# Taps in two halves, an earlier Sin, and four products per state block for the last four tiles of an S5 layer

## The reference, cut to what matters

```python
# 64 groups of 16 channels, 64 complex states per group
ab = exp(lam * dt);  bb = f * b                # zero-order hold
bu = einsum('blgp,gnp->blgn', u, bb)
st = scan of  s[t] = ab * s[t-1] + bu[t]       # complex, over 256 tokens
y  = einsum('blgn,gpn->blgp', st_re, cr) - einsum('blgn,gpn->blgp', st_im, ci)
y  = y + d_skip * h
g  = gelu(y);  out = g * sigmoid(g @ w_glu + b_glu)
```

## Time and profile before

| what | value |
|---|---|
| median of 3 runs | 1295.19 us |
| the profiled execution | 1296.42 us |
| its span, first to last instruction | 1294.6 us |
| TensorE matmul busy | 1247.5 us, 96% of the span |
| VectorE busy | 856.5 us, 66% |
| ScalarE busy | 605.4 us, 47% |
| chain that ended last | TensorE 86%, VectorE 5%, ScalarE 3%, DMA 3% |
| mean granted clock of TensorE | 0.979 |

### The profile page before, as it was taken

One profiled execution on the slowest core, in us unless ns is written; L12 is line 12 of the kernel. 1 busy time (PEld: TensorE's weight loads), 2 busy tenths in 40 slices (PEclk: granted clock), 3 DMA queues, 4 the chain that ended last, 5 costly groups with the idle time before them and its releaser, 6 DMA issues.

```text
span 1294.6 us, 25201 instructions
## 1 busy us (share of the span) xinstructions
PE 1247.5 (96%) x10872; PEld 1167.8 (90%) x10872; DVE 856.5 (66%) x1176; ACT 605.4 (47%) x778; POOL 51.8 (4%) x67
## 2 busy tenths in 40 slices
PE   5879999999999999999999999999999999999997
PEld 4667899999966489999999999999998999999997
DVE  6899678877547777768557565447469666666443
ACT  5854544433345465544345434336334545544342
POOL 5310000100000000000000000000000000000000
PEclk8968999999999999999999999999999999999998
DMA  9946568988742928654566554454454434655452
GB/s 261 311 152 204 200 227 287 333 290 270 223 156 93 298 93 280 208 194 155 166 199 195 163 179 162 155 177 155 145 167 149 146 131 131 196 194 188 146 179 73
DMA packets 219704, 247.01 MB, mean 191 GB/s; under 512 B 5872, under 2 KB 209088, under 8 KB 219616
## 3 DMA queue, kind: packets, MB, share of 16 engines
q1 hardware_dynamic: 211616, 218.63, 52.8%
q0 software_dynamic: 7648, 26.86, 6.1%
q10 hardware_dynamic: 352, 0.23, 0.1%
HBM read 244.66 MB, written 1.05 MB: 190 GB/s over the span
## 4 chain that ended last, share of the span: by engine, by line
PE 86%; DVE 5%; ACT 3%; DMA 3%; issue 1%; SPq 1%; DVEq 0%; ACTq 0%
PE PS L1749 85%; DMA RING<-in_ada_w 2%; SPq L441 1%; ACT PARTS L592 1%; DMA RING<-in_mla_w_uq 1%; DVE ARENA L1153 1%; DVE ARENA L1322 0%; DVE X L1157 0%; DMA RING<-in_w_in 0%; DVE ARENA L1350 0%; DVE PARTS L1011 0%; PE PS L2372 0%; DVE ARENA L1346 0%; DVE WL L1033 0%; PE PS L2088 0%
## 5 line engine op out<-in xcount | busy, mean ns | idle before, releaser
L1749 PE MATMUL PS<-PARTS 128*128 128x256 f32 (+3 forms) x3608 | 840.0, 283 | 0.0
L1749 PEld LDWEIGHTS PS<-PARTS 128*128 128x128 f32 (+1 forms) x3608 | 619.4, 189 | 1.4 <-issue 0.9
L1033 DVE TENSOR_TENSOR WL<-RING,PARTS 128x2048 fp32r<-128x2048 f32 (+2 forms) x189 | 387.3, 2053 | 241.1 <-ACT PARTS L592 240.6
L1749 PE MATMUL PS<-HH,WL 128*128 128x256 f32 (+3 forms) x1832 | 520.9, 284 | 2.0 <-DVE PARTS L1002 0.9
L1749 PE MATMUL PS<-HH,PARTS 128*128 128x256 f32 (+3 forms) x1832 | 518.6, 283 | 0.0
L592 ACT CAST PARTS<-RING 128x2048 fp32r<-128x2048 f32 (+2 forms) x189 | 324.1, 1717 | 306.5 <-DMA RING<-in_w_ffn_out 68.5
L1749 PEld LDWEIGHTS PS<-HH,WL 128*128 128x128 f32 (+1 forms) x1832 | 345.2, 188 | 7.9 <-issue 4.9
L1749 PEld LDWEIGHTS PS<-HH,PARTS 128*128 128x128 f32 (+1 forms) x1832 | 344.3, 188 | 0.4
L1749 PE MATMUL PS<-PARTS,WL 128*128 128x256 f32 (+1 forms) x832 | 236.9, 285 | 0.9 <-DVE PARTS L1648 0.5
L1749 PEld LDWEIGHTS PS<-PARTS,WL 128*128 128x128 f32 x832 | 158.2, 190 | 2.9 <-issue 2.1
L1749 PE MATMUL PS<-ARENA 128*32 128x63 f32 (+8 forms) x864 | 60.3, 279 | 2.8 <-DVE ARENA L1435 1.3
(11 more groups left out here) (349 smaller groups left out, 992.1 us busy)
## 6 DMA issues: line engine op xcount, KB each, us to landing
RING<-in_w_ffn_in SPq DMA_DIRECT2D x44, 1024.0 KB, 5.1
RING<-in_ada_w SPq DMA_DIRECT2D x32, 1024.0 KB, 8.7
RING<-in_ffn_w_gate SPq DMA_DIRECT2D x22, 1024.0 KB, 5.9
RING<-in_ffn_w_up SPq DMA_DIRECT2D x22, 1024.0 KB, 5.2
RING<-in_w_in SPq DMA_DIRECT2D x20, 1024.0 KB, 5.2
ARENA<-in_ada_w POOLq DMA_DIRECT2D x16, 1024.0 KB, 8.0
RING<-in_ffn_w_down SPq DMA_DIRECT2D x16, 768.0 KB, 4.8
RING<-in_w_ffn_out SPq DMA_DIRECT2D x16, 768.0 KB, 4.5
```

Source lines behind the costliest of these rows:

```text
L1033: V.tensor_tensor(WL[:, u % SLOTS, 0:w], RING[:, u % SLOTS, 0:w], WH[:, u % SLOTS, 0:w].bitcast(fp32), SUB)\
L1749: return nc.tensor.matmul(o, lhsT, rhs, start=start, stop=stop)
```

## The change

The fraction is made complete before VectorE waits for the modulation, and VectorE makes its absolute value; ScalarE takes two Sins and loads their table earlier. The taps are made and copied in two halves of four tiles, after `ada_rows(7)` and `(8)`; TensorE adds the diagonal as a product with the identity, and ScalarE copies all four distances. `ada_rows(9)` and the copy of its result come later. For the tiles 4 to 7 (`FOLD`) VectorE does not add the two parts: it leaves z * SIN, signed, in PS2 and z * COS in PC2, and `y_of` multiplies both by the same weights, 64 products in place of 32.

```diff
@@ k_out, ScalarE
-                act.wait_ge(S["k_ready"], 1)
                 act.wait_ge(S["kw_laid"], 2)
-                for q in range(4):
-                    rows = slice(32 * q, 32 * q + 32)
-                    ins = nc.scalar.copy(KWD[rows, :, 1:, rows], KTAPS[rows, :, 1:, :])
-                ins.then_inc(S["k_used"], 1)
+                for b in range(2):
+                    act.wait_ge(S["k_ready"], b + 1)
+                    for q in range(4):
+                        rows = slice(32 * q, 32 * q + 32)
+                        ins = nc.scalar.copy(KWD[rows, 4 * b:4 * b + 4, :, rows], KTAPS[rows, 4 * b:4 * b + 4, :, :])
+                    ins.then_inc(S["k_used"], 1)
@@ ScalarE's order
             b_blocks(1)
+            nc.scalar.preload_act_table_set("trig_and_small")
             row_copy(1)
...
             act.wait_ge(S["turn_cos"], 1)
-            nc.scalar.activation(by_pair(SIN), by_pair(COS), ACT.Sin, scale=2 * PI_IN)
-            link(nc.scalar.activation(by_pair(COS), by_pair(COS), ACT.Abs))
+            nc.scalar.activation(by_pair(SIN), by_pair(SIN), ACT.Sin, scale=2 * PI_IN)
             nc.scalar.activation(by_pair(COS), by_pair(COS), ACT.Sin, scale=-TWO_PI, bias=hpi).then_inc(S["turn_sin"], 1)
...
-                if kt == 3:
+                if kt == 4:
                     rows_copy()
@@ VectorE, the fraction
-            m, f = by_pair(SIN), by_pair(COS)
+            m, f = by_pair(COS), by_pair(SIN)
...
             link(V.tensor_tensor(f, f, m, SUB))
+            link(V.tensor_tensor(f, f, RMUL[:, :, :], ADD))
+            link(V.tensor_scalar(f, f, 0.5, -0.5, ALU.min, ALU.max))
...
             scaled(0, GS[:, 0, :], H, "norm_scaled")
-            link(V.tensor_tensor(f, f, RMUL[:, :, :], ADD))
-            V.tensor_scalar(f, f, 0.5, -0.5, ALU.min, ALU.max).then_inc(S["turn_cos"], 1)
+            V.scalar_tensor_tensor(m, f, -1.0, f, MUL, ALU.max).then_inc(S["turn_cos"], 1)
@@ scan, VectorE
                 link(ins)
+                if kt >= FOLD:
+                    for a in range(2):
+                        V.scalar_tensor_tensor(PS2[kt][:, :, a, :], z[:, :, a, :], 1.0 - 2.0 * a, SIN[:, :, kt, :], MUL, MUL)
+                        ins = V.tensor_tensor(z[:, :, a, :], z[:, :, a, :], COS[:, :, kt, :], MUL)
+                    ins.then_inc(S["s_done"], 1)
+                    return
@@ VectorE's order
             turned_in(4)
-            dve.wait_ge(S["k_used"], 1)
-            for q in range(4):
-                rows = slice(32 * q, 32 * q + 32)
-                ins = V.tensor_tensor(KWD[rows, :, 0, rows], KWD[rows, :, 0, rows], KTAPS[rows, :, 0, :], ADD)
-            ins.then_inc(S["k_used"], 1)
...
                 scan(kt)
-                states(kt)
@@ taps, TensorE
-                for kt in range(KT):
+                pe.wait_ge(S["kw_laid"], 1)
+                for kt in range(kt0, kt0 + 4):
...
                             ins = mm(KTAPS[rows, kt, :, :], BD[:, i, 4 * kt + q, :], CTD[:, :, i, kt, rows], i == 0, i == 1)
+                        if i == 0:
+                            for q in range(4):
+                                rows = slice(32 * q, 32 * q + 32)
+                                mm(KTAPS[rows, kt, 0, :], ident[rows, rows], KWD[rows, kt, 0, rows], False, False)
@@ y_of, TensorE
-                pe.wait_ge(S["k_used"], 2)
+                pe.wait_ge(S["k_used"], 1 if kt == 0 else 2)
...
-                            ins = mm(y[rows, 1:, t], CT4[t][i][:, kt, rows], PC2[kt][:, q, i, 0:NCH - 1], False,
-                                     t == CHUNK - 1 and i == 1)
+                            last = t == CHUNK - 1 and i == 1
+                            ins = mm(y[rows, 1:, t], CT4[t][i][:, kt, rows], PC2[kt][:, q, i, 0:NCH - 1], False, last and kt < FOLD)
+                            if kt >= FOLD:
+                                ins = mm(y[rows, 1:, t], CT4[t][i][:, kt, rows], PS2[kt][:, q, 1 - i, 0:NCH - 1], False, last)
@@ TensorE's order
-            taps()
             ada_rows(7)
             ada_rows(8)
+            taps(0)
+            taps(4)
             for kt in range(KT):
                 y_of(kt)
-                if kt == 0:
+                if kt == 2:
                     ada_rows(9)
```

More of the change, by code:

```diff
@@ L409, in x_of @@
             return X[:, :, TALL - N_TOK[n]:TALL]
+        FOLD = 4
         HP_LAST = {1: 1, 5: 2}
@@ L2117, in b_u, with taps @@
                 ins.then_inc(S["bu_ready"], 1)
-            def taps():
+            def taps(kt0):
                 pe.wait_ge(S["bd_zero"], 1)
```

## The result

The changed kernel takes 1300.32 us (median of 10 runs, 1295.28 to 1306.31) against 1294.54 for the kernel before, run beside it (10 runs, 1291.04 to 1298.37). The ratio is 1.0041, with a 95% interval of 1.0023 to 1.0058: some 5 us slower, where 3 us less was forecast and the range ended at 1296.0. The profiled run took 1300.51 us with a span of 1298.7 us, against 1296.42 and 1294.6.

What follows compares the result with a forecast made beforehand. VectorE bounds until 99.57 us, then TensorE. `y_of(0)` at 94.3 plus 27.1 us of outputs put the GLU at 121.4 against 124.64, 3.2 us less: 1292.0 us predicted; own range 1290 to 1294.5, with B and C 1288.0 to 1296.0.

Steps and rivals of the forecast that it cites:

- turned_in(0): VectorE's first turned tile after the Sin tables: begins at 64.9 us in place of 67.06, 2.15 us earlier.
- b_u(4..7): TensorE's products before the taps: start at 70.0 us, again take 13.9 us at the low clock, end at 83.9.
- the new form: VectorE's one scalar_tensor_tensor of 2048 behind the scaling: 2.37 us, from the add's 2.31 plus 0.06.
- the rows lifted the clock: TensorE's ada_rows(7) and (8) before the taps: start at 0.50, clock up 4.6 us later, 5.9 us in all.
- B: Rival at TensorE's rows before the taps: only the taps lift the clock; +0.4 us, 1295.6; chance 0.22.
- C: Rival at b_u(4..7): it runs at full clock, held or soon regained; 7.1 us less, 1288.1; chance 0.10.
- about 3.1 us at full clock: TensorE's 128 taps, 5.94 us nearly all at 0.50 before; with 1.0 us of diagonal products, 4.3 us for both halves.
- With 0.85 again: 27.1 us: TensorE's outputs stage: 26.3 us at full clock, plus the old 0.85 us of hole and small change.
- Rival D: At the outputs: low clock reaches into them, rising only 4.7 us into y_of(0); 4.7 us slower, 1299.9; chance 0.08.
- Carried to the end unchanged: From the first GLU product on, TensorE's order and inputs stay the same, so its 3.2 us shift holds to the end.
- 3.56 us and some 0.2 us of the two links fit into it: VectorE's add and clip, moved ahead, fit into its 4.23 us idle wait for the modulation rows, 0.4 us over.
- the fold at 1.6 us net: In the last four output tiles: added TensorE products against VectorE's saving, last tile ending at 120.6 instead of 119.0 us.

Runs made afterwards that it cites:

- e4: Changed kernel with the 32 extra products per folded tile replaced by 3 wide ones (only its time is of use): 1296.7 us, ratio 1.0004.
- e6: Changed kernel with the last two GLU units' weights loaded only after all outputs are made: 1305.15 us, ratio 1.0062.
- e1: Changed kernel without the fold, VectorE adding the state sums of all tiles: 1293.31 us, ratio 0.999 to the kernel before.
- e8: e1 with ScalarE's Sigmoid of the second GLU unit ahead of the cast of the first FFN weights: 1293.14 us, ratio 0.9972.
- e3: Changed kernel with ada_rows(9) back behind y_of(0) and its rows' copy behind the fourth GELU: 1299.35 us, ratio 1.0037.
- e11: The kernel before, unchanged, run once more: 1296.16 us, ratio 1.0017.
- e12: The kernel before with the Sigmoid of the second GLU unit ahead of the cast of the first FFN weights: 1294.57 us, ratio 1.0008.
- e2: The kernel before with the fold alone added: 1301.59 us, ratio 1.0046.
- e7: Changed kernel without TensorE's extra products with z * SIN, VectorE's fold work kept (only its time is of use): 1296.14 us, ratio 0.9992.
- e5: e1 with each state product of the last four tiles cut in two, of 31 and 32 columns: 1299.69 us, ratio 1.002.
- e9: Changed kernel with ada_rows(9) behind y_of(5), so the last GLU units' loads start later: 1298.48 us, ratio 1.0034.

## Why the prediction was wrong

**The steps that held.** With the start of the scaling of H as zero (51.88 us before, 50.98 after), `turned_in(0)` was forecast at 13.0 us and came at 13.1, `b_u(4..7)` at 18.1 and came at 18.1, its end was forecast at 32.0 and came at 31.9, the start of the taps at 37.9 and came at 37.2. The Abs is gone, the new form takes 2.37 us as worked out, `b_u` ran 13.90 us at 0.50 and the rows lifted the clock (5.43 us, forecast 5.9). Of the rivals B and C, neither happened.

**A term that was mis-sized.** "about 3.1 us at full clock" for the 128 taps. A round of 16 taps and 8 diagonal records starts every 0.77 us at 1.00; from the start of the 16 (90.99 us) to the next 8 it is 0.57 us, and 0.20 us are the 8. Eight rounds are 4.6 us of taps, not 3.1, and 1.6 us of diagonal, not 1.0. Against 5.94 us at 0.50 the full clock takes only a fifth off the taps, where half was forecast. Together they took 6.2 us, not 4.3. `y_of(0)` therefore lies 43.4 us behind the scaling, forecast 42.4; that it still came at 94.4 on the clock of the trace is the 0.9 us by which this execution's front started earlier.

**The step that failed** is "With 0.85 again: 27.1 us", the outputs. I had counted the one hole of 0.58 us as small change of the old kernel and carried it over, and asked of the fold only how long its products hold the array. The array time was nearly right: e4 and e6, which have it without the long stop, both take 28.3 us with 1.3 and 1.6 us of holes, so 26.7 to 27.0 without them, where the count said 26.3. What I did not ask is how TensorE gets its instructions. A folded tile has 272 instead of 144 instructions, a piece of the program per tile, and with the GLU's weights on the DMA engines that piece is late. It costs twice: after has 4.6 us of holes, e4 1.3, and behind the largest the clock is at 0.52 for 3.4 us, some 1.7 us more. 28.3 + 3.3 + 1.7 is 33.3 us; measured 32.9. This is a mechanism that no rival had. Rival D had its sign and one of its consequences, the low clock in the outputs, but from a late rise at their start; that did not happen, the clock was up before the taps, and that D's 1299.9 us lies next to the measured 1300.32 is luck.

**Carried to the end unchanged.** The shift was not. The FFN's first weights land 15.96 us behind the GLU's start instead of 14.46, and the third Sigmoid, queued behind their cast, makes TensorE wait, 1.36 us ahead of 145.98: 1.5 us for the stage. e1 has 1.1 us of it, and e8 takes 0.7 us back. Why the weights land later behind the new front stays open; e3, with `ada_rows(9)` at its old place, has 15.72 us.

**The cover of the front.** "3.56 us and some 0.2 us of the two links fit into it" was true of the one execution that I read, which had the longest wait of four (before, e11, e12, e2): 4.23, 3.55, 2.02 and 1.36 us. In e11 0.2 us would have stuck out, in e12 and e2 1.7 and 2.4 us. The four old fronts start their scaling at 51.88, 51.15, 49.58 and 48.65 us, the new ones always between 50.9 and 51.4. So the profiled span overstates the front's gain, 3.4 us (e1), of which the medians show 1.3 us with an interval (0.9979 to 1.0002) that takes in nothing at all.

**The balance by ratios,** times 1295 us: front alone -1.3 (e1); with the fold's VectorE part -1.0 (e7); with its array time +0.5 (e4); with its instructions +5.3 (after). The first two steps are within the uncertainty; the last, 4.8 us, is not. The forecast had the fold at 1.6 us net; it is 6 to 7.

**Open.** The holes of 0.6 to 1.2 us that end at 96 to 98.5 us in the other kernels with the new front (after has 0.32 and then 1.04 us) are the same thing by the two counts under e6, and a load runs beside each; but no run took that load away, so what they would be without it is not shown. Nor do the runs show why a piece then starts some 5 us behind the load's first packet (how the two are queued), nor how often the clock falls behind a hole from one execution to the next.

## What to carry to other kernels

Before moving work onto TensorE as many small products, count the instructions and not only the array time: 1.05 us in each of four tiles cost some 2 us in all as 3 wide products a tile (e4 against e1) and over 6 as 32 small ones (after against e1), because the program's own loads run beside the weights'. A stop for the program can be told from a wait: the instructions from one to the next are a multiple of 256, and it ends 1.2 to 1.6 us behind the landing of a piece. A hole put down to "issue" in a row of equal products is a question to the DMA queues, and where it is a fraction of a microsecond it is a warning: here 0.58 us became 4.6 us in all with 32 more products in each of four tiles. A cover read from one execution should be read from a second one before a gain is built on it.

## What the runs showed of the hardware

- The program comes in pieces of 16 KB by DMA queues of their own, all through the run (68 to 71 on the main one). TensorE went on 1.2 to 1.6 us behind the landing of one, at 33 stops of 33. Where a load filled the DMA engines (share 1.1) in the last 3 us before the piece started, it stood still for 0.1 us (e12) to 3.97 us (e5); where they had been idle that long, for 0.2 to 0.6 us or not at all, and for 1.72 us in e2, where VectorE had a part in it.
- In eight traces the first piece of the program behind the start of a weight load starts 4.9 to 5.2 us behind the load's first packet; without the load, in e6, it starts at 107.54 us where after has 111.55.
- With such a hole the clock may fall or not: it fell to 0.50 with 1.71 us (e7), 2.13 (e3), 3.26 (after) and 3.97 us (e5, 1.1 us before the hole's end), and stayed at 1.00 with 1.77 (e8), 1.78 (e1) and 2.19 us (e9). The length of the hole alone does not decide it.
- The low clock has a price that depends on the work: 64 state products take 1.02 us at 1.00 and 1.84 us at 0.50 (e7, 118.76 to 120.60), a tap takes 36 ns at 1.00 (16 in 0.57 us, after) and 45 ns nearly all at 0.50 (128 in 5.77 us, start to start, before). Counts are records of the trace.
- Half the columns are not half the time: a state product of 63 columns takes 16 ns, one of 31 or 32 columns 11 ns (e5).
